# Another order of the seven products of a tile pair, with all of their sums taken out of PSUM by VectorE, in a one-layer hybrid decoder step

## The chip, the cores and the metric

The kernel runs on one core of a Trainium2 chip. The metric is the device time of one execution in microseconds, as the median of several runs. Times of single instructions and waits come from one profiled execution.

## What is computed

One inference step of one decoder layer for a prompt of 2048 tokens with 16 meta tokens, and for 8 sample sequences of 8 tokens. All is fp32, with a model width of 1024.

```python
def _in_proj(x, g_pre, w_in, b_in):
    h = _rmsnorm(x, g_pre)
    p = jnp.einsum('btd,dc->btc', h, w_in) + b_in
    return jnp.split(p, np.cumsum(IN_WIDTHS)[:-1].tolist(), axis=-1)
...
def _mlstm_chunk(carry, inp):
...
    Wqk = W * jnp.einsum('blhd,bshd->bhls', q, k)
    num = a[..., None] * jnp.einsum('blhd,bhde->bhle', q, C0) + jnp.einsum('bhls,bshe->bhle', Wqk, v)
...
def _merge(x, att, hm, za, om, zm, ga, gb, w_pa, w_pb, w_out, g_post):
    y_a = att * jax.nn.silu(za)
    y_m = jax.nn.sigmoid(om) * hm * jax.nn.silu(zm)
    merged = jax.nn.sigmoid(ga) * jnp.einsum('btc,cd->btd', y_a, w_pa) + jax.nn.sigmoid(gb) * jnp.einsum('btc,cd->btd', y_m, w_pb)
    out = jnp.einsum('btd,de->bte', merged, w_out)
    return x + _rmsnorm(out, g_post)
```

Branch A is sliding-window attention with sinks (16 query heads, 4 key heads), branch B an mLSTM with 4 heads of width 256, in chunks of 128 tokens.

## The kernel before

**Split numbers.** Every projection is computed from numbers in two parts: an fp32r upper part and the rest, the lower part. A product of two such numbers is three matmuls: upper by upper, upper by lower, lower by upper. ScalarE writes the upper part (a copy), VectorE or GpSimd subtracts it from the number to give the lower part.

**First stage** (`attention`). The tokens lie in 17 tiles (tile 0: meta and sample rows). Four passes over them, one for each key head, make 68 slots m = 0 to 67, each with the projection of the next tile, the scores, softmax and values of this one. In pass 0 h is made, split and stored in DRAM as `hh_t`. From slot 17 on the split h of tile m+2 is loaded in SP's slot m (`load_split`, L283, two DMAs of 512 KB) into one of two buffers, behind what SP did in the slot before. GpSimd makes beside that the sums of operands for the later pairs (`operand_sums`, stored at L603 as `sh_t`), sixteen sets of weight differences (stored at L590) and the lower parts of the first weight units (`early_units`). In its last slots TensorE makes the first four products of the stream (`first_products`, L1552 to L1554). A barrier of all engines closes the stage.

**Stream** (`stream`). Ten passes ZM, H0 to H3, GA, PA, GB, PB, OUT, each with a weight of 1024 x 1024. An item is tile 0 alone (4 products) or a pair of tiles (7 products), so a pass has 4 + 8 x 7 = 60 products, and the stream 600, numbered q. A product is an operand of 128 x 512 by a weight block of 512 x 512, 12 matmuls of 512 columns (L2790, L2792, L2793). The two tiles of a pair times the four blocks of the weight would be 8 products. A scheme of the Strassen and Winograd kind makes 7 of them out of sums of operands and differences of weight blocks (T1 to T4), and sums the results. P1 and P2 give c11, the left half of row 0; c12 is its right half, c21 and c22 are row 1. Before, the order is P1, P5, P6, P2, P7, P3, P4. bank_first takes P1 and P2, bank_third P5 and then P3, bank_second P6, then P7 afresh, then P4 on top.

Who takes what out before: VectorE takes t1 (after P1), u2 (P6), c11 (P2), c12 (P3) and c21 (P4); ScalarE copies p5 (L2464) and p7 (L2469); GpSimd adds in `second_sums` (L2264, L2267) and `last_sum` (L2275, c22). `c` has three lines: line 2 for tile 0, lines 0 and 1 for the rows of a pair. Before a line is written, `wait_line` waits until its former contents are stored (ZM, GA, PA, GB), used by the mixer (head passes), transposed (PB) or added by GpSimd (OUT).

**Operands.** The passes called STREAMED (ZM, the head passes, GA, GB) load split operands from DRAM, three products ahead. PA, PB and OUT (SUMMED) load raw tiles. There ScalarE makes the upper parts (L2329), VectorE the lower ones (L2507), GpSimd the operand sums (`make_sums`, L2209 to L2221).

**Weights.** A pass needs 28 units of 128 x 512, split at 2 for each product from 6 products before the pass to 8 products into it (`SPLITS_AT`): ScalarE the upper part (L2336), VectorE (L2512) or GpSimd (L2179) the lower one. Units of T1 to T4 are read from `difs_t`. For passes 2 to 9 GpSimd makes the differences in the stream (`differences`, L2186 to L2192), in 64 steps spread by `DIF_AT` over products 1 to 331. SP loads (L1991) and stores them (L1995).

**Mixer.** In a head pass each tile is turned (`TURN`: transposes of q and k), scored one product later (`SCORE`) and mixed two products later (`MIX`). All engines walk the same list of products in order. The order within one engine at one product is that of the code.

## Time and profile before

| | us |
|---|---|
| median of 3 runs | 2965.0 (2960.8 to 2971.6) |
| the profiled execution | 2957.5 |
| its span, first to last instruction | 2955.7 |
| TensorE busy | 2758.2 (93%) |
| VectorE busy | 1551.9 (53%) |
| ScalarE busy | 1014.8 (34%) |
| GpSimd busy | 1232.4 (42%) |
| mean granted TensorE clock | 0.976 |

PE is TensorE, PEld its weight loads, DVE VectorE, ACT ScalarE, POOL GpSimd, and SPq the queue of SyncE, which issues DMAs. The first stage lasts to about 941 us. The passes of the stream begin at 924 (ZM), 1124, 1362, 1596, 1829 (H0 to H3), 2062 (GA), 2234 (PA), 2403 (GB), 2572 (PB) and 2758 us (OUT). L12 is line 12 of the kernel before.

### The profile page before, as it was taken

Reading aid. Unit: us, or ns where it says so; the run is one execution under the profiler, and the core shown is the slowest. Engines: PE = TensorE matmul, PEld = TensorE weight load, DVE = VectorE, ACT = ScalarE, POOL = GpSimd, SP = SyncE. Lnnn points to the kernel's source line nnn. Section 1 sums busy time; section 2 is a strip of 40 time slices with the busy share of each in tenths; the row PEclk is TensorE's granted clock in tenths of the full one; section 3 lists DMA queues with packets and bytes.
Section 4 is the critical chain, followed back from the end, with each engine's and each line's share of the span. In section 5 each row is a group of like instructions: output and inputs, shape, how many; then the busy total and the mean of one; then the engine's idle time right before and its main releaser. Section 6 shows DMA issues by size and latency. Waiting matters only on the chain. (4 is left out here: it accounts for less than half of the span.)

```text
span 2955.7 us, 46918 instructions
## 1 busy us (share of the span) xinstructions
PE 2758.2 (93%) x15620; PEld 2306.7 (78%) x15620; DVE 1551.9 (53%) x3788; ACT 1014.8 (34%) x2451; POOL 1232.4 (42%) x1386
## 2 busy tenths in 40 slices
PE   6999898899886998999999999999999999999798
PEld 5888787788775875887788788788887878778686
DVE  5775555455443114446446446545317551487887
ACT  5774333333333002224124123223214341343443
POOL 3343433433444333234234224324425452377777
PEclk9999999999898999999999999999999999999999
DMA  8664555454456998888888788778987577966643
GB/s 305 236 205 144 166 187 184 154 181 158 160 173 209 306 332 291 272 281 278 252 278 300 242 268 290 251 232 276 335 302 260 186 256 249 307 213 221 200 154 145
DMA packets 410017, 697.49 MB, mean 236 GB/s; under 512 B 31778, under 2 KB 176551, under 8 KB 409748
## 3 DMA queue, kind: packets, MB, share of 16 engines
q1 hardware_dynamic: 394628, 649.42, 66.4%
q10 hardware_dynamic: 12432, 35.76, 3.4%
q0 software_dynamic: 2720, 9.32, 1.0%
q8 instruction: 128, 2.10, 0.3%
q14 instruction: 109, 0.89, 0.1%
HBM read 526.87 MB, written 169.48 MB: 236 GB/s over the span
## 5 line engine op out<-in xcount | busy, mean ns | idle before, releaser
L2790 PE MATMUL bank_second<-w_all,a_all 128*128 128x512 f32 x704 | 287.3, 408 | 17.8 <-POOL w_all L2179 10.2
L2793 PE MATMUL bank_second<-w_all,a_all 128*128 128x512 f32 x704 | 276.0, 392 | 0.0
L2792 PE MATMUL bank_second<-w_all,a_all 128*128 128x512 f32 x704 | 275.1, 391 | 0.0
L2275 POOL TENSOR_TENSOR st_c<-st_p 128x512 f32<-128x512 f32 x80 | 107.7, 1347 | 331.1 <-PE st_bank_u L2842 257.8
L2790 PE MATMUL bank_first<-w_all,a_all 128*128 128x512 f32 x560 | 226.0, 404 | 19.3 <-DVE st_c L2531 16.3
L2264 POOL TENSOR_TENSOR st_t<-st_u,st_db 128x512 f32<-128x512 f32 x56 | 73.6, 1314 | 394.1 <-DVE st_u L2558 394.0
L2793 PE MATMUL bank_first<-w_all,a_all 128*128 128x512 f32 x560 | 219.2, 391 | 0.0
L2792 PE MATMUL bank_first<-w_all,a_all 128*128 128x512 f32 x560 | 218.9, 391 | 0.0
L316 PE MATMUL bank_third<-w_all,a_all 128*128 128x256 f32 (+1 forms) x480 | 158.3, 330 | 59.2 <-DMA a_all<-hh_t 58.9
L2405 ACT ACTIVATE mx_qkt<-st_bank_t 128x512 f32<-128x512 f32 x68 | 40.7, 599 | 445.5 <-PE st_bank_t L2813 445.5
L307 PE MATMUL bank_first<-w_all,a_all 128*128 128x384 f32 x544 | 189.3, 348 | 0.0
L2790 PE MATMUL bank_third<-w_all,a_all 128*128 128x512 f32 x440 | 178.8, 406 | 7.8 <-issue 3.5
L309 PE MATMUL bank_first<-w_all,a_all 128*128 128x384 f32 x544 | 182.0, 335 | 0.0
L308 PE MATMUL bank_first<-w_all,a_all 128*128 128x384 f32 x544 | 182.0, 335 | 0.0
L923 ACT ACTIVATE at_sm<-at_sm,at_nmx 128x208 f32<-128x208 f32 x272 | 124.5, 460 | 166.4 <-DVE at_nmx L1131 166.3
L769 POOL TENSOR_TENSOR at_vbc<-at_qkv,at_ones 64x64 f32<-64x64 f32 x68 | 23.8, 349 | 370.3 <-PE at_bank_po L1475 370.3
L2507 DVE TENSOR_TENSOR a_all<-h_raw,a_all 128x512 fp32r<-128x512 f32 x99 | 134.6, 1359 | 76.5 <-ACT a_all L2329 75.9
L2790 PEld LDWEIGHTS bank_second<-w_all,a_all 128*128 128x128 f32 x704 | 132.9, 189 | 52.6 <-POOL w_all L2179 9.2
L2793 PE MATMUL bank_third<-w_all,a_all 128*128 128x512 f32 x440 | 172.2, 391 | 0.0
L2792 PE MATMUL bank_third<-w_all,a_all 128*128 128x512 f32 x440 | 171.5, 390 | 0.0
L2512 DVE TENSOR_TENSOR w_all<-st_waiting,w_all 128x512 fp32r<-128x512 f32 x129 | 122.8, 970 | 76.7 <-ACT w_all L2336 76.3
L2336 ACT ACTIVATE w_all<-st_waiting 128x512 fp32r<-128x512 f32 x188 | 114.1, 628 | 128.8 <-DMA st_waiting<-difs_t 59.5
(383 smaller groups left out, 7760.5 us busy)
## 6 DMA issues: line engine op xcount, KB each, us to landing
a_all<-hh_t SPq DMA_DIRECT2D x284, 512.0 KB, 5.6
a_all<-sh_t SPq DMA_DIRECT2D x224, 512.0 KB, 5.2
st_waiting<-difs_t SPq DMA_DIRECT2D x152, 256.0 KB, 6.9
h_raw<-l_blocks_in SPq DMA_DIRECT2D x64, 512.0 KB, 7.0
difs_t<-h_raw SPq DMA_DIRECT2D x64, 512.0 KB, 6.9
st_waiting<-l_blocks_in SPq DMA_DIRECT2D x108, 256.0 KB, 6.7
hh_t<-a_all SPq DMA_DIRECT2D x34, 512.0 KB, 6.1
st_raw<-y_t ACTq DMA_DIRECT2D x16, 1024.0 KB, 6.4
```

Of the source, the lines that this page charges most:

```text
L307: nc.tensor.matmul(out, hi[:, j], k.w_hi[:, j, col:col + n], start=(j == 0), stop=False)
L308: nc.tensor.matmul(out, hi[:, j], k.w_lo[:, j, col:col + n], start=False, stop=False)
L309: last = nc.tensor.matmul(out, lo[:, j], k.w_hi[:, j, col:col + n], start=False, stop=(j == KT - 1))
L316: nc.tensor.matmul(out, hi[:, j], k.w_hi[:, j, col:col + n], start=(j == 0), stop=False)
L923: nc.scalar.activation(sm[:, g, :], sm[:, g, :], ACT.Exp, bias=nmx[:, g:g + 1], scale=HD ** -0.5, accum_out=rs[:, g:g + 1]).then_inc(exp_r ...
L2275: G.tensor_tensor(c[:, 1, LW:D], p5[:, :], p7[:, :], ALU.add).then_inc(c22_ready, 1)
L2336: A.activation(unit_half(v, 0), unit_view(v), ACT.Copy).then_inc(k.upper_done, 1)
L2507: V.tensor_tensor(k.a_all[:, 1, q % NA], operand(q), hi, ALU.subtract).then_inc(a_lo, 1)
L2512: V.tensor_tensor(unit_half(v, 1), unit_view(v), unit_half(v, 0).bitcast(F32), ALU.subtract).then_inc(lower_done_dve, 1)
L2790: T.matmul(bank_view(bank, at), hi, weight_row(k, at, 0, t), start=fresh and t == 0, stop=False, skip_group_check=True)
L2792: T.matmul(bank_view(bank, at), hi, weight_row(k, at, 1, t), start=False, stop=False, skip_group_check=True)
L2793: last = T.matmul(bank_view(bank, at), lo, weight_row(k, at, 0, t), start=False, stop=t == KH - 1, skip_group_check=True)
```

## The change

- The pair's order is P1, P6, P5, P7, P2, P3, P4, with the weight order to match. P7 is accumulated in bank_second on top of P6.
- VectorE takes out all: t2 and t1 from P1 (t1 by ScalarE in PA, PB and OUT), u2 from P6, u3 and c22 after P7, c11, c12, c21. P3 waits for c22. The two ScalarE copies and GpSimd's `second_sums`, `last_sum` and `make_db` are gone.
- `make_sums` is moved from GpSimd to VectorE as it stands.
- In the first stage ScalarE loads the split h, of tile m+3 in slot m, behind the four at_pt copies, and the first four operands of the stream as well.
- The early weight units come one slot earlier. The last four no longer wait for the lower parts of the others.
- The bias of ZM is loaded before the barrier into the first half of h_raw, and VectorE takes the right half of tile 0 out there into the second half.
- The 64 difference steps are moved to products 64 to 299 and their DMAs to ScalarE's queue. A load waits for the landing of the store two steps before, a store for GpSimd's step.
- The tiles of a head pass are turned earlier: a pair's at its P3 and at the next P1 (before: at the next P1 and the next P2).
- The units of the ZM pass are split 5 products later, and the first six units of a next pass are loaded 6 products later.
- On VectorE the outputs of the mixer now stand before its next weights, queries and gates.

```diff
-NEEDED = (T3, B22, B11, B21, T1, T2, T4)
-RELEASED = (B11, T1, T2, B21, T3, B22, T4)
+NEEDED = (T3, B22, B11, B21, T2, T1, T4)
+RELEASED = (B11, T2, T1, T3, B21, B22, T4)
...
-            if m < KVH * NT - NT + 2:
+            if m < KVH * NT - NT + 1:
...
             def slot(a, t, m, u, half):
-                if m + 2 == NT:
-                    sp.wait_ge(hh_out[0], 32 * (NT // 2 + 1))
-                    sp.wait_ge(hh_out[1], 32 * (NT // 2))
-                if NT <= m + 2 < KVH * NT:
-                    load_split(sp, k, m + 2, u, (m + 2) % NT)
-                elif m + 2 == KVH * NT:
+                if m == KVH * NT - 3:
+                    sp.wait_ge(pair_out[1], 32 * (NPT // 2 + 1))
+                    sp.dma_start(k.h_raw[:, 0].rearrange("p j n -> p (j n)"), k.l_bias[0:1].to_broadcast([P, D])).then_inc(k.first_bias_in, 16)
+                if m == KVH * NT - 1:
                     sp.wait_ge(proj_a, m + 1)
-                    sp.wait_ge(pair_out[1], 32 * (NPT // 2 + 1))
-                    for q in range(2):
-                        load_operand(sp, k, q)
-                elif m + 2 > KVH * NT:
-                    sp.wait_ge(proj_a, m + 1)
-                    sp.wait_ge(k.lower_done, EARLY - KH)
                     for e in range(EARLY - KH, EARLY):
                         load_early(e)
-                    for q in range(2, 4):
-                        load_operand(sp, k, q)
...
                     nc.scalar.activation(pt[:, g, :], pbank(g)[:, 0:2 * P], ACT.Copy).then_inc(pt_ready, 1)
+                n = m + 3
+                if n == NT:
+                    act.wait_ge(hh_out[0], 32)
+                    act.wait_ge(hh_out[1], 32 * (NT // 2))
+                elif n == NT + 1:
+                    act.wait_ge(hh_out[0], 32 * (NT // 2 + 1))
+                if NT <= n < KVH * NT:
+                    load_split(act, k, n, n % 2, n % NT)
+                elif KVH * NT <= n < KVH * NT + 2:
+                    act.wait_ge(proj_a, n - 1)
+                    act.wait_ge(pair_out[1], 32 * (NPT // 2 + 1))
+                    for q in (0, 1) if n == KVH * NT else (2, 3):
+                        load_operand(act, k, q)
...
             all_steps(KVH, slot)
+            dve.wait_ge(k.prod, 2)
+            dve.wait_ge(k.first_bias_in, 16)
+            dve.wait_ge(pair_out[1], 32 * (NPT // 2 + 1))
+            V.tensor_tensor(k.h_raw[:, 1, KH:KT].rearrange("p j n -> p (j n)"), k.bank_first[:, :],
+                            k.h_raw[:, 0, KH:KT].rearrange("p j n -> p (j n)"), ALU.add).then_inc(k.first_ready, 1)
...
-P1, P5, P6, P2, P7, P3, P4 = range(7)
-PAIR_BLOCK = (B11, T1, T2, B21, T3, B22, T4)
+P1, P6, P5, P7, P2, P3, P4 = range(7)
+PAIR_BLOCK = (B11, T2, T1, T3, B21, B22, T4)
...
-DIF_AT = {c: 1 + (c - DIF_FIRST) * 21 // 4 for c in range(DIF_FIRST, N_DIF)}
+DIF_AT = {c: N_PROD * H0 + 4 + ((c - DIF_FIRST) * 9 // 2 if c < DIF_FIRST + 8 else 37 + (c - DIF_FIRST - 8) * 18 // 5) for c in range(DIF_FIRST, N_DIF)}
...
     if t < 3:
-        return b + (6, 13, 16)[t]
-    return b + N_SINGLE + N_PAIR * ((t + 1) // 2) + (0 if t % 2 else 3)
+        return b + (4, 11, 12)[t]
+    return b + N_SINGLE + N_PAIR * (t // 2) + (5 if t % 2 else 0)
...
+            def load_dif(c):
+                if c - DIF_FIRST >= 2:
+                    act.wait_ge(dif_out[c % 2], 16 * ((c - DIF_FIRST) // 2))
...
+            def store_dif(c):
+                act.wait_ge(dif_step, 4 * (c - DIF_FIRST + 1))
...
+                if q + 3 in DIF_NOW:
+                    load_dif(DIF_NOW[q + 3])
+                if q - 3 in DIF_NOW:
+                    store_dif(DIF_NOW[q - 3])
                 mixer_first(q)
...
                 if j == P1 and s in STREAMED:
...
+                    V.tensor_tensor(t2[:, :], bank_x[:, :], bias_of(s)[:, LW:D], ALU.add).then_inc(t2_ready, 1)
+                    V.tensor_tensor(t1[:, :], bank_x[:, :], bias_of(s)[:, 0:LW], ALU.add).then_inc(t1_ready, 1)
...
+                elif j == P7:
+                    dve.wait_ge(c22_ready, m)
+                    V.tensor_tensor(u3[:, :], bank_y[:, :], t2[:, :] if s in STREAMED else t1[:, :], ALU.add).then_inc(u3_ready, 1)
+                    wait_line(dve, g, 1, 1)
+                    dve.wait_ge(u3_ready, m + 1)
+                    V.tensor_tensor(c[:, 1, LW:D], bank_z[:, :], u3[:, :], ALU.add).then_inc(c22_ready, 1)
...
-                    fresh = j in (P1, P5, P6, P7)
+                    fresh = j in (P1, P5, P6)
...
                     elif j == P3:
-                        pe.wait_ge(p5_ready, m + 1)
+                        pe.wait_ge(c22_ready, m + 1)
                     elif j == P4:
-                        pe.wait_ge(p7_ready, m + 1)
+                        pe.wait_ge(u3_ready, m + 1)
```

## Rows read from the trace of the kernel before

**Rows 1.** Busy time by stretch: length; PE, PEld, DVE, ACT, POOL; clock; DMA share, GB/s.
```profile
234.00:924.00 690.00, 611.68 (x5009) 545.46 (x5007) 357.05 (x1482) 262.98 (x902) 264.29 (x498) 0.94 0.52 167
...
1596.00:1829.00 233.00, 231.65 (x1124) 187.42 (x1123) 120.83 (x270) 63.64 (x151) 80.28 (x82) 1.00 0.83 270
...
2572.00:2758.00 186.00, 178.03 (x842) 147.12 (x841) 154.80 (x126) 81.04 (x145) 134.55 (x91) 1.00 0.67 229
2758.00:2956.00 198.00, 169.99 (x737) 139.38 (x735) 153.26 (x141) 83.70 (x155) 146.47 (x76) 0.94 0.44 157
```
**Rows 2.** Timeline of TensorE, first matmuls of two products in ZM: start, duration.
```profile
1033.22 0.39 PE L2790 MATMUL bank_second<-w_all,a_all 128*128 128x512 f32 x1
...
1035.94 0.39 PE L2790 MATMUL bank_first<-w_all,a_all 128*128 128x512 f32 x1
```
**Rows 3.** Waits of TensorE, whole run: us in total, times, longest.
```profile
PE bank_third L316 <- DMA a_all<-hh_t: 58.9, 25, 5.9
PE bank_first L2790 <- DVE st_c L2531: 16.3, 1, 16.3
...
PE bank_second L2790 <- POOL w_all L2179: 10.2, 3, 7.7
...
PE st_bank_t L2740 <- POOL st_c L2241: 7.6, 2, 6.1
...
PE bank_third L2790 <- DMA a_all<-sh_t: 6.6, 2, 4.2
...
PE bank_first L1552 <- issue: 4.4, 1, 4.4
```
**Rows 4.** Line L898, once a slot: from 234 to 924 us, then 472 to 493.
```profile
L898 ACT ACTIVATE at_qt<-at_bank_pt x52: 384/385/387, 234.2 to 917.8; 128x256 f32<-128x256 f32 x52
...
L898 ACT ACTIVATE at_qt<-at_bank_pt x2: 385/386/386, 472.8 to 492.6; 128x256 f32<-128x256 f32 x2
```
**Rows 5.** Timeline of ScalarE, two slots; in brackets idle time before, and its releaser.
```profile
602.03 0.39 ACT L898 ACTIVATE at_qt<-at_bank_pt 128x256 f32<-128x256 f32 x1 [2.41 <-PE at_bank_pt L1414]
...
613.06 0.39 ACT L898 ACTIVATE at_qt<-at_bank_pt 128x256 f32<-128x256 f32 x1 [1.93 <-PE at_bank_pt L1414]
```
**Rows 6.** Waits of SP's queue from 234 to 924 us.
```profile
SPq L603 <- POOL h_raw L835: 194.0, 17, 20.5
```
**Rows 7.** Line L283, the loads of split h, from 234 to 924 us.
```profile
DMA to landing us min/median/max: 3.3/6.0/9.1
```
**Rows 8.** Timelines of TensorE and of SP from 940 to 963 us.
```profile
957.77 0.77 PE L2790 MATMUL bank_first<-w_all,a_all 128*128 128x512 f32 x1 [16.31 <-DVE st_c L2531]
...
943.15 2.97 SPq L2001 DMA_DIRECT2D st_waiting<-difs_t  x6
```
**Rows 9.** DMA issues of the page: count, KB, median us from issue to landing.
```profile
st_waiting<-difs_t SPq DMA_DIRECT2D x152, 256.0 KB, 6.9
...
difs_t<-h_raw SPq DMA_DIRECT2D x64, 512.0 KB, 6.9
...
zm_t<-st_c SPq DMA_DIRECT2D x17, 512.0 KB, 7.7
...
gb_t<-st_c SPq DMA_DIRECT2D x17, 512.0 KB, 6.4
```
**Rows 10.** Eviction of P1 (busy, mean ns); timelines of VectorE and GpSimd in PB.
```profile
L2551 DVE TENSOR_TENSOR st_t<-bank_first,st_bias 128x512 f32<-128x512 f32 x56 | 38.7, 691 | 96.9 <-PE bank_first L2793 96.9
...
2653.04 2.30 DVE L2507 TENSOR_TENSOR a_all<-st_raw,a_all 128x512 fp32r<-128x512 f32 x1
...
2659.93 0.68 DVE L2507 TENSOR_TENSOR a_all<-h_raw,a_all 128x512 fp32r<-128x512 f32 x1
...
2652.00 2.79 POOL L2241 TENSOR_TENSOR st_c<-st_c,st_e 128x1024 f32<-128x1024 f32 x1 [2.01 <-DVE st_c L2518]
```
**Rows 11.** Transposes in PB (timeline); GpSimd's add in OUT (busy, mean ns).
```profile
2657.35 0.60 PE L2740 MATMUL st_bank_t<-ident,st_c 128*128 128x128 f32 x4
...
L2247 POOL TENSOR_TENSOR st_e<-st_c,st_e 128x1024 f32<-128x1024 f32 x17 | 43.3, 2547 | 37.1 <-DVE st_c L2592 34.0 <-ACT st_p L2464 3.0
```

More of the change, by code:

```diff
@@ L605, in load_early @@
             def load_early(e):
+                if e == 2 * KH:
+                    for out in dif_out:
+                        sp.wait_ge(out, 16 * KH)
                 sp.dma_start(early_place(e), unit_source(k, EARLY_ORDER[e]).rearrange("p (t n) -> p t n", n=P)).then_inc(early_in[e % 4], 16)
@@ L1763, in stream @@
         sums = k.h_raw[:, :, :, :].rearrange("p u (s j) n -> p (u s) j n", j=KH)
-        t1, u2, p5, p7 = (sb(name, [P, LW]) for name in ("t1", "u2", "p5", "p7"))
-        bias, db = sb("bias", [P, D]), sb("db", [P, LW])
+        t1, t2, u2, u3 = (sb(name, [P, LW]) for name in ("t1", "t2", "u2", "u3"))
+        bias = sb("bias", [P, D])
+        first = k.h_raw[:, 1].rearrange("p j n -> p (j n)")
         c = sb("c", [P, 3, D + 1])
@@ L2530, in evict_single @@
                     wait_bias(s)
-                    V.tensor_tensor(c[:, 2, cols], bank[:, :], bias[:, cols], ALU.add).then_inc(ready, 1)
+                    V.tensor_tensor(c[:, 2, cols] if g else first[:, cols], bank[:, :], bias_of(s)[:, cols], ALU.add).then_inc(ready, 1)
                 elif s == OUT:
@@ L2580, in evict_pair, with make_sums @@
                     wait_line(dve, g, 1, 0)
-                    V.tensor_tensor(c[:, 1, 0:LW], bank_y[:, :], u2[:, :], ALU.add).then_inc(c21_ready, 1)
+                    dve.wait_ge(t1_ready, m + 1)
+                    V.tensor_tensor(c[:, 1, 0:LW], bank_y[:, :], t1[:, :], ALU.add).then_inc(c21_ready, 1)
+            def make_sums(g, which):
+                n = sums_before(g)
+                if g == N_ITEM * PA and which == 0:
+                    for out in dif_out:
+                        dve.wait_ge(out, 16 * ((N_DIF - DIF_FIRST) // 2))
+                if which == 0 or is_single(g):
+                    wait_raw(dve, g)
+                if is_single(g):
+                    if which == 0:
+                        dve.wait_ge(a_lo, sums_taken(g, 0))
+                        V.tensor_tensor(sums[:, 0], raw_block(g, 0, 0), raw_block(g, 0, 1), ALU.add).then_inc(sums_ready, 1)
+                elif which == 0:
+                    dve.wait_ge(a_lo, sums_taken(g, 0))
+                    V.tensor_tensor(sums[:, 0], raw_block(g, 1, 0), raw_block(g, 1, 1), ALU.add).then_inc(sums_ready, 1)
+                    dve.wait_ge(sums_ready, n + 1)
+                    dve.wait_ge(a_lo, sums_taken(g, 1))
+                    V.tensor_tensor(sums[:, 1], sums[:, 0], raw_block(g, 0, 0), ALU.subtract).then_inc(sums_ready, 1)
+                else:
+                    dve.wait_ge(a_lo, sums_taken(g, 2))
+                    V.tensor_tensor(sums[:, 2], raw_block(g, 0, 0), raw_block(g, 1, 0), ALU.subtract).then_inc(sums_ready, 1)
+                    dve.wait_ge(sums_ready, n + 2)
+                    dve.wait_ge(a_lo, sums_taken(g, 3))
+                    V.tensor_tensor(sums[:, 3], raw_block(g, 0, 1), sums[:, 1], ALU.subtract).then_inc(sums_ready, 1)
             def norm_row(g, row):
@@ L2695, in _ @@
                             evict_single(g, j)
+                h = META.get(q - 1)
+                if h is not None:
+                    meta(h)
+                n = MIX.get(q - 1)
+                if n is not None:
+                    outputs(n)
                 n = SCORE.get(q - 1)
@@ L2700, in _ @@
                     split_operand(q + 3)
+                if 0 <= q < Q_ALL:
+                    s, i, j = place(q)
+                    g = N_ITEM * s + i + 1
+                    if g < G_ALL and g // N_ITEM in SUMMED:
+                        if j == (1 if i else 0):
+                            make_sums(g, 0)
+                        if j == (4 if i else 2):
+                            make_sums(g, 1)
                 n = TURN.get(q - 1)
```

187 lines of the change are left out of this document (48 added, 139 removed).

## The prediction

> **What bounds the kernel now.** Three views in this order. The busy table by stretch [rows 1] says where TensorE is the limit: in the middle of the run it is busy 231.65 of 233 us (a head pass) at full clock, but only 612 of 690 us in the first stage, at 0.94 of the clock, 178 of 186 us in the PB pass and 170 of 198 us in the OUT pass with its tail. So a product pass has nothing to give in its steady part: two products of one pair start at 1033.22 and 1035.94, 2.72 us apart, matmul behind matmul [rows 2], and a change can only harm there. What there is to gain is idle time, and the list of TensorE's waits [rows 3] says whose it is: 58.9 us in 25 waits for the split h (hh_t) in the attention stage, 16.3 us once at the start of the stream, 10.2 and 7.6 us for GpSimd at pass starts, 6.6 us for operand loads, 4.4 us once before the first products.
>
> The 58.9 us cost more than themselves. The ScalarE copy L898 runs once a slot: 52 times from 234.2 to 917.8 [rows 4], 51 slots in 683.6 us. A slot without a wait takes 613.06 - 602.03 = 11.03 us [rows 5]; a first-tile slot without one 492.6 - 472.8 = 19.8 us [rows 4], and there are 3. 48 x 11.03 + 3 x 19.8 = 588.8, so 94.8 us are lost: the waits and the half clock (1.2 GHz) behind them. Why are the loads late? SP's own waits [rows 6]: it stands 194 us in 17 waits before the pair stores at L603, for GpSimd, and the hh_t load is queued behind them. The landing itself takes 3.3 to 9.1 us, median 6.0 [rows 7].
>
> **Split h from ScalarE's queue.** The load of tile m+3 is now issued in ScalarE's slot m behind the four at_pt copies; its TensorE wait (projection of m+2) precedes the transposes those copies read, so ScalarE does not stop for it. That is before the end of slot m; the tile is first needed at the start of slot m+2, so a whole clean slot (11.03 us) lies between. Two issues, estimated at 0.5 us each from SP's six in 2.97 us [rows 8], then at most 9.1: 10.1 us, so it arrives. The issues stand before the at_gt copy; ScalarE then sits idle for 1.93 us before the next L898 copy [rows 5], so 1 us fits. What is next late is nothing I can see: a slot without the wait is all TensorE. I take -90 of the -94.8 us, bounds -60 and -95. At one end DMA traffic pressed into shorter slots makes some loads late, at the other none.
>
> In front of this stands a rule. The Trainium skill, "DMA: Bandwidth & Descriptors", section "Issuing engines are not separate DMA queues", says that DMAs of all issuing engines share the same 16 DMA engines and that spreading them saves only the time of initiating. By that rule alone the 90 us would be near zero; it hangs on whether landing or issue is late, and rows 6 and 7 show the issue.
>
> **The early units one slot earlier** remove the 4.4 us before the first products [rows 3], which are w_early lowered by GpSimd behind a difference set: -4 (0 to -8).
>
> **Start of the stream.** TensorE ends at 957.77 - 16.31 = 941.46 and begins again at 957.77 [rows 8], when VectorE has read both banks of the single tile, which waits for the bias behind four lowerings. Now one half of that tile is taken out before the barrier, the bias is already there, and P1 and P6 have weights and operands. The third product needs T1, loaded after the barrier: six issues from 943.15 [rows 8], then the median of 6.9 us of the loads of difference units [rows 9] and a split and lowering of some 2 us: about 951 to 952. By then two products (5.4 us) are done, where before none was: it corresponds to a start at about 946. -11 (-7 to -14).
>
> **Weight differences out of the ZM pass, onto ScalarE's queue.** Relief for the operand loads, which wait 6.6 us on one row [rows 3] and a few more on others, around the burst of state and unit loads: -6 (0 to -12). The 64 differences now fall on products 64 to 299. For most, the load of c+2 stands one product behind the store of c on the same engine and waits for its landing, 6.9 us too [rows 9]; a head-pass product averages 233/60 = 3.9 us, so ScalarE is held some 3 us. Queued behind are the copies and exponentials of the mixer. I price it at 0: ScalarE is busy 64 of 233 us [rows 1], and it runs ahead of TensorE in the products between two tiles. Upper bound in the rivals.
>
> **VectorE takes all sums from PSUM.** Per streamed pair three evictions more (t2, u3, c22), else two, at 691 ns each [rows 10] (PSUM operand, so the same beside GpSimd); gone are ScalarE's two copies and GpSimd's sums. 56 x 3 + 24 x 2 = 216 x 0.69 = 149 us on an engine that is 52% busy; hidden, if they come in time. Each is waited for with one product between, 2.72 us, and the worst slot has two, 1.4 us: on time. In PA, PB and OUT 4 operand sums a pair come too, 33 x 0.69 = 23 us a pass. VectorE is busy 155 of 186 us in PB [rows 1], which looks full. But an a_all lowering there takes 2.30 us beside GpSimd's L2241 and 0.68 with GpSimd idle [rows 10]: GpSimd loses six pieces of 512 a pair, at half of L2247's 2547 ns for 1024 [rows 11] some 61 of its 135 us in PB, and with them about half of what lengthens VectorE. I work with 155 + 23 + 11 - 35 = 154 us: no new bound.
>
> What is new is **what c22 waits for.** It must find its line free, VectorE waits in order, and P3 waits for it. (a) PB: the line is freed by the transposes of the former pair, which TensorE makes after P2, the product just before P3. They start at 2657.35, the first four take 0.60 us [rows 11]; only behind them can VectorE write c22 (0.69 + about 0.1 us), with TensorE idle: 0.8 x 7 pairs = +5.6 us, sure. u3, P2's eviction and the lowerings queued behind c22 have some 7 us of room. (b) OUT: the line is freed by GpSimd's add (2547 ns) [rows 11] behind the norm of the row (1.3 to 2.1 us) behind one lowering: 0.69 + 0.16 + 1.3 + 2.55 = 4.7 us of the 4.75 that are there, up to 1.6 us too late: +4 (0 to 11). (c) ZM, GA, GB: by the store of the line, issued behind an operand load, some 0.5 us into the third product; it may take 3 x 2.72 - 0.5 - 0.69 = 7.0 us, and takes 7.7 in ZM and 6.4 in GB [rows 9]; without differences ZM should be like GB: +2 (0 to 8).
>
> **Order in the head passes.** A pair's tiles are turned at P3 and at the next P1, mixed two products later; tile 2 one product behind tile 1. VectorE's slot after P1 then holds two evictions, the outputs and the queries, near 4.5 us, in a slot of 2.72 us plus a mix and a turn: fits. T1's lowering meets the queries of tile 0. +3 (0 to 12).
>
> **Pass starts PB and OUT.** GpSimd loses the sums before its lowerings: 10.2 + 7.6 = 17.8 us of waits [rows 3], and the OUT stretch stands at 0.94 of the clock [rows 1]. VectorE still has lowerings, sums and evictions there at once. -12 (+4 to -22).
>
> **The sum.** -90 - 4 - 11 - 6 - 12 + 5.6 + 4 + 2 + 3 = -108. The profiled execution took 2957.5 us (span 2955.7 and 1.8 around it), so 2849. It lies 7.5 us under the median of the runs, 2965.0; the same 108 off that is **2857 us**.
>
> **Rivals.**
> 1. The hh_t loads stay late on the other queue, because the landing grows. Against: 6.0 us median against more than 11 us of room. For: traffic of 690 us falls into some 600. Half of the gain gone: 2857 + 45 = 2902; all of it, as by the rule of the skill's page: 2947. Chance 0.14, nearly all on the half.
> 2. VectorE becomes the bound in PA, PB and OUT: the lengthening stays (155 + 34 = 189 us in PB against 186) and c22's wait of some 3.5 us a pair adds to it. That is 189 + 8 x 3.5 = 217 against 186 in PB and OUT, and nothing gained at their starts: +31 x 2 + 12 = 74, so 2931. Chance 0.06.
> 3. Slower than before: ScalarE's hold at the difference loads. 56 of them, 3 us each, is 168 us; if all reach TensorE, 2857 + 168 = 3025. It decides at the point where ScalarE comes to a load less than 3 us before the copy of the turned tile is due. The profile speaks against it, as two or three products of each pair ask nothing of ScalarE. A third of it would still be faster. Chance 0.04.
> 4. The change does not do what it says (a wait I read wrongly puts the load back behind GpSimd, gains and losses cancel): 2957 to 2974. Chance 0.02.
>
> My forecast keeps 0.74, its own range 2828 to 2888. For 8 in 10 I take in half of rival 1: **2822 to 2905**. Within 0.3% (9 us) a measurement of this kernel can't tell a change from none. Faster 0.94, same 0.02, slower 0.04.
>
> **What the profile after would show.** The wait for hh_t gone, L898 at 11.0 us a slot, the first stage done near 825; the idle time at the stream's start 2 to 3 us, then some 2 to 3 more before the third product; in PB idle pieces of 0.8 us before P3 released by VectorE; lowerings of a_all mostly at 0.69 us; PA, PB and OUT no longer than 170, 190 and 190 us. It is wrong if hh_t waits remain at a third of the tiles, if head passes last over 240 us, or if TensorE waits for VectorE in most pairs of ZM, GA and GB.

## The result and the profile after

The changed kernel takes 2919.9 us (median of 4 runs, 2916.6 to 2923.5), the kernel before beside it 2968.3. The ratio is 0.984 with a 95% interval of 0.9815 to 0.9865. So it is 48 us faster, where I had forecast 108, and 2919.9 lies above my range of 2822 to 2905. Direction right, size wrong.

The head of the page after:

```profile
span 2914.8 us, 46458 instructions
...
PE 2763.5 (95%) x15620; PEld 2298.4 (79%) x15620; DVE 1636.7 (56%) x4103; ACT 936.0 (32%) x2291; POOL 762.2 (26%) x1064
```

TensorE's waits over the whole run (us in total, times, longest; from here on line numbers are those of the kernel named):

```profile
PE bank_third L2760 <- DVE st_c L2497: 27.4, 21, 3.4
PE st_bank_s L2772 <- ACT mx_yt L2379: 12.5, 4, 3.1
...
PE st_bank_n L2839 <- DVE mx_wqk L2564: 10.0, 4, 4.9
PE bank_third L2760 <- POOL w_all L2177: 9.2, 2, 4.9
```

The 58.9 us for split h [rows 3] are gone, and so are the 16.3 us at the start of the stream. In their place stand waits of the new order: L2497 writes c22, L2379 takes out the transposed y of a tile, L2564 makes a tile's weights. The ScalarE copy once a slot (L898 before, L892 now) for the first stage:

```profile
L892 ACT ACTIVATE at_qt<-at_bank_pt x52: 373/384/384, 233.8 to 841.7; 128x256 f32<-128x256 f32 x52
```

That is 607.9 us for the 51 slots that took 683.6 [rows 4]; 588.8 would be clean. The table sets lengths side by side, each from the first matmul of a pass to that of the next, as span of the rows by stretch. The last two columns are kernels of the experiments.

| us | before | after | first half alone | after, repaired |
|---|---|---|---|---|
| 51 slots | 683.6 | 607.9 | 608.2 | 607.1 |
| last slot copy to the stream's product 4 | 40.0 | 17.7 | 18.8 | 19.4 |
| rest of ZM | 166.5 | 164.7 | 162.7 | 165.7 |
| four head passes | 937.3 | 969.2 | 935.4 | 935.3 |
| GA, PA, GB | 510.2 | 516.1 | 513.5 | 523.4 |
| PB | 186.0 | 193.1 | 189.0 | 184.2 |
| OUT | 186.7 | 201.2 | 186.7 | 184.6 |
| span | 2955.7 | 2914.8 | 2858.3 | 2864.5 |

Items 0 and 1 below are the first eleven products of a head pass, items 2 and 3 the next fourteen, each sum over the four passes, read from the first matmuls of their products in TensorE's timeline.

So 98 us were gained by product 4 of the stream (75.7 in the slots, 22.3 behind them), and some 57 of them were given back from there to the end: 31.9 in the head passes, 14.5 in OUT, 7.1 in PB and 5.9 in GA, PA and GB are 59.4, less the 1.8 that the rest of ZM is shorter. The second head pass and OUT by stretch, after (columns as in [rows 1]):

```profile
1264.99:1508.41 243.42, 234.15 (x1124) 188.62 (x1122) 130.33 (x294) 54.94 (x134) 61.36 (x75) 0.99 0.85 279
...
2702.45:2903.67 201.22, 178.35 (x737) 141.24 (x735) 140.49 (x180) 73.82 (x136) 55.65 (x26) 0.94 0.43 147
```

TensorE sits idle for 9 us in the head pass, where before a head pass had 1.35 [rows 1], and the clock is under 1.00. VectorE is busy 130 of 243 us, so it is not the bound. Where in these passes does the time go?

**Tiles 1 and 2 of a head pass.** Rows of TensorE, VectorE and ScalarE from 1084 us, product 13 of H0; the same idle time of 3.1 us stands there in all four head passes.

```profile
1088.61 1.03 PE L2808 MATMUL st_bank_n<-mx_cn,mx_qat 128*128 128x257 f32 x4
...
1094.05 0.41 PE L2772 MATMUL st_bank_s<-ident,mx_y 128*128 128x128 f32 x2 [3.12 <-ACT mx_yt L2379]
...
1096.25 0.63 PE L2762 MATMUL bank_second<-w_all,a_all 128*128 128x512 f32 x1
```
```profile
1090.27 0.42 DVE L2577 TENSOR_TENSOR mx_qat<-mx_qkt,mx_rows 128x256 f32<-128x256 f32 x1 [3.92 <-PE st_bank_n L2809]
...
1092.32 0.48 DVE L2622 SCALAR_TENSOR_TENSOR mx_y<-st_bank_n,mx_den,mx_tz 128x256 f32<-128x256 f32 x1
```
```profile
1090.97 0.51 ACT L2349 ACTIVATE mx_kw<-st_c,spare 128x256 f32<-128x256 f32 x1 [4.27 <-PE st_bank_u L2812]
1092.92 0.42 ACT L2366 ACTIVATE mx_to<-st_c 128x256 f32<-128x256 f32 x1 [1.43 <-DVE mx_y L2622]
1093.24 0.40 ACT L2367 ACTIVATE mx_tz<-mx_z 128x256 f32<-128x256 f32 x1
1093.55 0.36 ACT L2379 ACTIVATE mx_yt<-st_bank_s 128x256 f32<-128x256 f32 x1
```

Nobody is busy here; it is a chain. Tile 2 is turned one product behind tile 1. VectorE's queries of tile 2 (L2577) wait for the mix of tile 1, ScalarE's k (L2349) for its state update, its tanh (L2366) for VectorE's y, and its copy of the y of the tile before (L2379) stands behind all of that, with TensorE waiting for it. Behind the idle time the matmuls of 512 columns take 0.63 us instead of 0.39: the granted clock is 0.61 in the mean from 1094.0 to 1098.4 us and 1.00 again from 1098.6 on. That is the half clock, 1.2 GHz, for some 3 us.

**ScalarE held by a difference load.** ScalarE's rows around the start of H2, then TensorE's:

```profile
1504.74 0.40 ACTq L2266 DMA_DIRECT2D difs_t<-h_raw  x1
...
1514.14 0.38 ACTq L2262 DMA_DIRECT2D h_raw<-l_blocks_in  x1
1514.56 0.31 ACT L2333 ACTIVATE mx_wexp<-mx_wexp 128x128 f32<-128x128 f32 x1 [3.33 <-DMA difs_t<-h_raw]
```
```profile
1515.31 1.22 PE L2808 MATMUL st_bank_n<-mx_cn,mx_qat 128*128 128x257 f32 x2 [3.91 <-DVE mx_wqk L2564]
```

The store is issued at 1504.74 and the load that waits for its landing at 1514.14; the exponential queued behind the load starts after 3.33 us of idle time, then come VectorE's weights, then TensorE. The stores (L2266) in the whole run:

```profile
DMA to landing us min/median/max: 2.9/7.3/15.5
```

In the head passes ScalarE stands idle for 39.4 us in 11 such waits, the longest 6.3 us. That is less than the 56 waits of 3 us of my bound, but not nothing.

**c22 in PB and OUT.** One pair of each, VectorE (in OUT with GpSimd) and TensorE:

```profile
2584.49 0.60 PE L2711 MATMUL st_bank_s<-ident,st_c 128*128 128x128 f32 x4
2585.96 0.47 PE L2760 MATMUL bank_third<-w_all,a_all 128*128 128x512 f32 x1 [0.88 <-DVE st_c L2497]
```
```profile
2585.12 0.69 DVE L2497 TENSOR_TENSOR st_c<-bank_third,st_u 128x512 f32<-128x512 f32 x1 [2.91 <-PE st_bank_s L2711]
```
```profile
2757.93 2.50 DVE L2432 TENSOR_TENSOR a_all<-h_raw,a_all 128x512 fp32r<-128x512 f32 x1
...
2761.14 1.29 DVE L2555 SCALAR_TENSOR_TENSOR st_c<-st_c,st_small,st_e 128x1024 f32<-128x1024 f32 x1
...
2764.90 0.69 DVE L2497 TENSOR_TENSOR st_c<-bank_third,st_u 128x512 f32<-128x512 f32 x1 [1.87 <-POOL st_e L2215]
```
```profile
2762.51 2.36 POOL L2215 TENSOR_TENSOR st_e<-st_c,st_e 128x1024 f32<-128x1024 f32 x1 [2.63 <-DVE st_c L2555]
```
```profile
2765.74 0.47 PE L2760 MATMUL bank_third<-w_early,a_all 128*128 128x512 f32 x1 [1.86 <-DVE st_c L2497]
```

In PB c22 starts when the transposes have ended, 0.88 us too late, in all seven pairs from the second on. In OUT it starts when GpSimd's add has ended, and TensorE waits 1.9 us in six pairs and 0.8 in the last.

### The profile page after: what moved, and what is told of

Its sections match the earlier page's. It is cut to its first block and busy times, and to the rows that moved or that the text cites. A ratio compares the mean times of both kernels' runs of the same rounds, so it can differ in the third digit from the quotient of the medians.

```text
span 2914.8 us, 46458 instructions
## 1 busy us (share of the span) xinstructions
PE 2763.5 (95%) x15620; PEld 2298.4 (79%) x15620; DVE 1636.7 (56%) x4103; ACT 936.0 (32%) x2291; POOL 762.2 (26%) x1064
## 5 line engine op out<-in xcount | busy, mean ns | idle before, releaser
L2760 PE MATMUL bank_second<-w_all,a_all 128*128 128x512 f32 x736 | 298.9, 406 | 2.0 <-DVE st_u L2491 0.9
L2763 PE MATMUL bank_second<-w_all,a_all 128*128 128x512 f32 x736 | 288.6, 392 | 0.0
L2762 PE MATMUL bank_second<-w_all,a_all 128*128 128x512 f32 x736 | 288.3, 392 | 0.0
L2177 POOL TENSOR_TENSOR w_all<-st_waiting,w_all 128x512 fp32r<-128x512 f32 x59 | 80.1, 1359 | 626.4 <-ACT w_all L2274 626.4
L2760 PE MATMUL bank_third<-w_all,a_all 128*128 128x512 f32 x464 | 190.3, 410 | 29.9 <-DVE st_c L2497 12.9
L2760 PE MATMUL bank_first<-w_all,a_all 128*128 128x512 f32 x496 | 197.5, 398 | 4.1 <-DMA a_all<-first_t 2.0
L2763 PE MATMUL bank_first<-w_all,a_all 128*128 128x512 f32 x496 | 194.6, 392 | 0.0
L2762 PE MATMUL bank_first<-w_all,a_all 128*128 128x512 f32 x496 | 194.6, 392 | 0.0
L2184 POOL TENSOR_TENSOR h_raw<-h_raw 128x256 f32<-128x256 f32 x64 | 48.5, 757 | 538.4 <-DMA h_raw<-l_blocks_in 538.2
L2763 PE MATMUL bank_third<-w_all,a_all 128*128 128x512 f32 x464 | 184.6, 398 | 0.0
L2762 PE MATMUL bank_third<-w_all,a_all 128*128 128x512 f32 x464 | 184.4, 397 | 0.0
L2760 PEld LDWEIGHTS bank_second<-w_all,a_all 128*128 128x128 f32 x736 | 139.6, 190 | 34.5 <-issue 6.8
L2763 PEld LDWEIGHTS bank_second<-w_all,a_all 128*128 128x128 f32 x736 | 139.1, 189 | 30.1
L2762 PEld LDWEIGHTS bank_second<-w_all,a_all 128*128 128x128 f32 x736 | 139.5, 190 | 26.8
L316 PE MATMUL bank_third<-w_all,a_all 128*128 128x256 f32 (+1 forms) x480 | 147.3, 307 | 0.2 <-POOL a_all L297 0.2
L2494 DVE TENSOR_TENSOR st_u<-bank_second,st_t 128x512 f32<-128x512 f32 x80 | 55.2, 690 | 157.3 <-PE bank_second L2763 157.3
```

The costliest lines, as they stand in the source:

```text
L316: nc.tensor.matmul(out, hi[:, j], k.w_hi[:, j, col:col + n], start=(j == 0), stop=False)
L2177: G.tensor_tensor(unit_half(v, 1), unit_view(v), unit_half(v, 0).bitcast(F32), ALU.subtract).then_inc(k.lower_done, 1)
L2184: G.tensor_tensor(d[:, R11], d[:, R12], d[:, R11], ALU.subtract).then_inc(dif_step, 1)
L2494: V.tensor_tensor(u3[:, :], bank_y[:, :], t2[:, :] if s in STREAMED else t1[:, :], ALU.add).then_inc(u3_ready, 1)
L2760: T.matmul(bank_view(bank, at), hi, weight_row(k, at, 0, t), start=fresh and t == 0, stop=False, skip_group_check=True)
L2762: T.matmul(bank_view(bank, at), hi, weight_row(k, at, 1, t), start=False, stop=False, skip_group_check=True)
```

## The experiments

Theory: the first half of the change (queue of split h, early units, bias ahead of the barrier) gives what I forecast, and the second half gives 57 us back in the places above. Rival: VectorE, with three more evictions a pair, is simply late. Ratios are against the kernel before, times are medians of 4 runs, and what is said of single passes comes from the profiled one of them.

**1. The load of split h alone.** In the kernel before:

```diff
-                if m + 2 == NT:
...
-                    load_split(sp, k, m + 2, u, (m + 2) % NT)
...
+                n = m + 3
...
+                if NT <= n < KVH * NT:
+                    load_split(act, k, n, n % 2, n % NT)
                 act.wait_ge(gate_tr, m + 1)
```

> The kernel before, with one edit of the change: ScalarE loads the split h of tile m+3 in slot m, behind the four at_pt copies; all else stays, SP's loads of the first operands too. My theory: this edit alone carries the gain of the first stage. L898 comes 17 to 67 in about 600 us instead of 672.6, TensorE's waits for hh_t there go from 58.9 us to under 5, nothing is given back in the stream, so the kernel is 75 us faster: 2890 (2880 to 2900). That would make it faster than the whole change. Rival A (the gain needs the other edits of the stage as well): 2905 to 2935. Rival B (the landing is what is late, so another queue saves only the issuing time): 2955 to 2965.

Measured: 2880.4 us, ratio 0.971 (0.969 to 0.974). That is 10 us better than I expected, and this one edit is faster than the whole change by 40 us. Its slots, and its loads from 234 to 850 us:

```profile
L893 ACT ACTIVATE at_qt<-at_bank_pt x52: 375/384/385, 233.5 to 839.1; 128x256 f32<-128x256 f32 x52
```
```profile
L283 ACTq DMA_DIRECT2D a_all<-hh_t x98: 366/465/1630, 242.3 to 815.5; - x98
...
DMA to landing us min/median/max: 3.2/5.0/10.2
```

605.6 us for 51 slots, 78.0 less, and no wait for hh_t in them. A landing takes 5.0 us in the median against 6.0 [rows 7], with a longest of 10.2: hardly faster, but no longer issued late. The Trainium skill ("DMA: Bandwidth & Descriptors", section "Issuing engines are not separate DMA queues") says that another issuing engine saves only the initiating. The landings here agree. But what "initiating" was worth is 78 us. By the rows it was late because it stood behind another wait, 194 us in 17 times [rows 6]; the loads left on SP's queue but ahead of those waits, which would show this without another queue, were not run.

**2. The differences back on SP's queue**, in the kernel after (SP's side is shown; the same lines are taken out of ScalarE's loop):

```diff
                     next_operand(q + LOADED_AHEAD)
+                if q + 3 in DIF_NOW:
+                    load_dif(DIF_NOW[q + 3])
+                if q - 3 in DIF_NOW:
+                    store_dif(DIF_NOW[q - 3])
```

> The kernel after, with the loads and stores of the weight differences in the stream issued by SP, behind the operand load, instead of ScalarE. My theory: ScalarE's hold at a difference load, which waits for the landing of a store, is what makes TensorE wait 3.9 us at product 180, 3.6 us at product 245 and 2.7 us of the 4.9 us at product 126. These go, with the half clock behind them: head passes 0 to 8 us shorter, 2905 (2900 to 2912). Rival A (VectorE with its three more evictions is late in the head passes, whatever ScalarE does): the same waits stay, 2920. Rival B (SP, held at the same waits, now brings the operands late): slower than 2920, with waits for hh_t and sh_t in the head passes.

Measured: 2917.2 us, ratio 0.983 (0.981 to 0.986): too high for my theory, and level with the change. The waits at products 180 and 245 are gone (3.9 to 1.0 us, and 3.6 to none), and the head passes take 963.0 us instead of 969.2. But at product 126 TensorE still waits 3.7 us. SP's queue says why:

```profile
1280.39 0.69 SPq L1636 DMA_DIRECT2D a_all<-sh_t  x1
1287.69 0.38 SPq L2007 DMA_DIRECT2D h_raw<-l_blocks_in  x1
```

For 7 us SP issues nothing, standing at the same wait, and behind it the weight units of H1 come late. In the head passes SP stands 124.6 us in 42 of these waits. So the hold comes from the short distance between the two commands, and moving them from ScalarE's queue to SP's only changed what stood behind it.

**3. Tile 1 turned one product earlier**, in the kernel after:

```diff
-        return b + (4, 11, 12)[t]
+        return b + (4, 10, 12)[t]
```

> The kernel after, with tile 1 of each head pass turned one product earlier (10 instead of 11 products into the pass), so that tiles 1 and 2 are two products apart instead of one. My theory: turned one product apart, tile 2's queries wait for tile 1's mix and then everything behind them runs in series; that is the idle time of 3.1 us at product 13 of each of the four head passes, and the half clock behind it. Both go: item 2 of a head pass falls from 31.7 to about 27 us, 2900 (2896 to 2906). Rival A (the time is bound to the 16 matmuls of the mixer in that product, or moves into the sample updates at products 7 to 10): 2918 to 2922. Rival B (VectorE is overloaded there): the wait stays with VectorE as its releaser, 2915 to 2920.

Measured: 2905.1 us, ratio 0.979 (0.976 to 0.981). The waits for L2379 are gone altogether, item 2 takes 26.5 us instead of 31.5 to 31.7 in all four passes, and the head passes 952.2 us instead of 969.2: 17.0 (the medians are 14.9 apart). VectorE's work is the same in both, so the chain was the cause.

**4. PB's row 1 transposed behind P7**, in the kernel after:

```diff
-                    g = ended(q - 1 - 3 * row, row)
+                    g = ended(q - 1 - 2 * row, row)
                     if g is not None and g // N_ITEM == PB:
                         transposes(g, row)
```

> The kernel after, with the transposes of row 1 in PB made one product earlier, behind P7 instead of behind P2. My theory: c22 then finds its line free before TensorE is through with P2, so the 0.88 us ahead of P3 go in all seven pairs, and with them the rest of what the pair takes over 20.85 us: 7 x 1.1 = 8 us, 2912. PB falls from 193 to about 185 us. Rival A (GpSimd's add for row 1 ends later than P7, and TensorE waits for it instead): PB unchanged or longer, 2920 or more. Rival B (the 0.88 us are VectorE's own length for u3 and c22 behind P2's lowerings, not the line): the wait stays, 2918 to 2920.

Measured: 2910.1 us, ratio 0.981 (0.979 to 0.983). PB by stretch (length; PE, PEld, DVE, ACT, POOL; clock, DMA share, GB/s), after and then here:

```profile
2509.38:2702.45 193.07, 182.06 (x841) 149.12 (x840) 141.93 (x178) 73.57 (x129) 63.48 (x42) 0.98 0.67 222
```
```profile
2509.12:2694.72 185.60, 179.75 (x842) 148.26 (x840) 141.95 (x178) 73.34 (x129) 63.24 (x42) 0.99 0.69 229
```

7.5 us, and pairs of 20.9 us as in the kernel before.

**5. OUT's row 1 normed into the bias buffer**, in the kernel after:

```diff
-                V.scalar_tensor_tensor(out=c[:, at, 0:D], in0=c[:, at, 0:D], ...
+                V.scalar_tensor_tensor(out=bias[:, :] if row else c[:, at, 0:D], in0=c[:, at, 0:D], ...
...
-                    G.tensor_tensor(e[:, row], c[:, at, 0:D], e[:, row], ALU.add)
+                    G.tensor_tensor(e[:, row], bias[:, :] if row else c[:, at, 0:D], e[:, row], ALU.add)
```

> The kernel after, where in OUT the norm of row 1 writes its result into the bias buffer, free in that pass, and GpSimd adds from there. Line 1 is free when VectorE's norm is through (before c22 in its own order), not when GpSimd's add of 2.4 to 2.5 us behind it is. My theory: that add is what c22 waits for in OUT. The 1.9 us ahead of P3 in six pairs, and the half clock that follows, go: six pairs of 21.4 to 23.1 us become 19.0 to 19.3, the last one 19.3: 20 us, 2900 (2896 to 2906). Rival A (VectorE itself is late there, with norm, two lowerings and two evictions): pairs of 20 to 21 us, 2908 to 2914. Rival B (the wait is for ScalarE's mean square): unchanged.

Measured: 2905.2 us, ratio 0.980 (0.979 to 0.982). OUT takes 184.4 us instead of 201.2, its pairs 19.7 us instead of 21.4 to 23.1 (19.0 in the kernel before). 16.8 us of the 20: the wait ahead of P3 is 0.1 us. Why 0.7 us a pair remain is open.

**6. Operand sums back on GpSimd**, in the kernel after: `make_sums` with `G` for `V`, at its old place in GpSimd's loop.

> The kernel after, with the operand sums of PA, PB and OUT made by GpSimd again, at the places they had in the kernel before. My theory: moving them to VectorE paid, because GpSimd's work beside VectorE lengthens VectorE's lowerings. Back on GpSimd the a_all lowerings go from 0.7 back to about 2 us, VectorE comes later to c22, and P3 waits longer: PB and OUT together 5 to 20 us longer, 2925 to 2940. Rival (the lengthening costs nothing, VectorE has room): 2917 to 2923, PB and OUT within 2 us.

Measured: 2926.1 us, ratio 0.988 (0.985 to 0.991), 6 us more than the kernel after, with runs from 2922.8 to 2937.7 us beside 2916.6 to 2923.5. The profiled run is the slowest of these, at 2937.7, so the lengths of its passes say too much: PA, PB and OUT are 2.8, 2.0 and 9.8 us longer in it. In PB and OUT the lowerings of a_all from raw tiles (busy, mean ns), after and then here:

```profile
L2432 DVE TENSOR_TENSOR a_all<-st_raw,a_all 128x512 fp32r<-128x512 f32 x52 | 37.7, 725 | 33.6 <-ACT a_all L2252 33.6
```
```profile
L2465 DVE TENSOR_TENSOR a_all<-st_raw,a_all 128x512 fp32r<-128x512 f32 x52 | 71.6, 1376 | 37.7 <-ACT a_all L2285 37.6
```

The lowerings of sums (h_raw) in the same passes hardly differ, 1221 ns against 1293. In PB VectorE is busy 141.9 us with the sums and 154.6 without them: with more to do it is through sooner. Moving the sums to VectorE seems to have paid, by some 6 us, but the two kernels' intervals (0.9815 to 0.9865, and 0.985 to 0.991) overlap. The Trainium skill ("SBUF — State Buffer", section "SBUF: two separate sides") says that VectorE reading two SBUF inputs and GpSimd lock each other out for a whole instruction; 1376 against 725 ns agrees in direction.

**7. Difference loads later, steps 4.5 products apart**, in the kernel after:

```diff
-DIF_AT = {c: N_PROD * H0 + 4 + ((c - DIF_FIRST) * 9 // 2 if c < DIF_FIRST + 8 else 37 + (c - DIF_FIRST - 8) * 18 // 5) ...
+DIF_AT = {c: N_PROD * H0 + 4 + (c - DIF_FIRST) * 9 // 2 ...
...
-                if q + 3 in DIF_NOW:
-                    load_dif(DIF_NOW[q + 3])
+                if q + 1 in DIF_NOW:
+                    load_dif(DIF_NOW[q + 1])
```

> The kernel after, differences still on ScalarE's queue, but each difference load is issued 1 product ahead of its step instead of 3, and the steps stand 4.5 products apart all along (now 3.6 for most). From a store to the load of the same buffer it is then 5 products instead of 1.2 to 3, more than a landing of 7 to 10 us, so that nobody is held. My theory: ScalarE's holds are gone, and SP isn't held instead as in the run with the loads on SP. Items 0 and 1 of the four head passes, 224.7 us together (216.5 with the loads on SP), fall to about 210, the kernel to 2906 (2900 to 2912). Rival A (what is late there is the traffic itself, 345 GB/s at a DMA share of 0.95 in 1265 to 1305): 216 to 225, 2915 to 2920. Rival B (GpSimd is now the one that waits for the landing, and its unit lowerings come late at pass starts): waits for GpSimd's w_all, 2915 to 2930.

Measured: 2917.2 us, ratio 0.984 (0.982 to 0.986). Half right. Items 0 and 1 of the head passes fall to 209.0 us and the head passes to 953.2, 16.0 less, and ScalarE waits for no landing of a difference store there any more. Two things were changed at once, the distance and the spacing of the steps; run 9 parts them. But GA takes 185.7 us instead of 176.3, since the last steps now fall there. VectorE in a pair of GA, and TensorE behind it:

```profile
2031.55 0.69 DVE L2497 TENSOR_TENSOR st_c<-bank_third,st_u 128x512 f32<-128x512 f32 x1 [3.66 <-DMA ga_t<-st_c]
```
```profile
2032.39 0.56 PE L2760 MATMUL bank_third<-w_all,a_all 128*128 128x512 f32 x1 [2.57 <-DVE st_c L2497]
```

c22 waits for the store of its line, in seven pairs of GA, 10.8 us in all. That is a weak spot of the new order: it needs each store landed within a pair, and difference traffic beside it (329 GB/s here, 286 after) breaks that.

**8. The first half of the change alone**: edit 1, and to it the early units, the first operands from ScalarE's queue, bias and right half of tile 0 ahead of the barrier, the units of ZM 5 products later, and the differences out of ZM (on SP's queue, 4.5 products apart; in the change they are on ScalarE's and mostly 3.6 apart). The pair's order and all behind it as before.

> The kernel before with the first half of the change: split h and the first four operands from ScalarE's queue, early units one slot earlier, bias of ZM and right half of tile 0 before the barrier, units of ZM 5 products later, and the differences out of ZM, but on SP's queue, one every 4.5 products from product 64. The order of the pair's products, who takes the sums out, the tiles' turns, the operand sums and all of PB and OUT stay as before. My theory: all of the gain is in this half, and all that is given back is in the other: 2880 of the run with the load alone, less 16 at the start of the stream and 2 to 6 in ZM: 2860 (2852 to 2868), the head passes 233 to 237 us as before. Rival A (differences pressed into fewer products hold SP and make operands and units late, in this order of products too): head passes 236 to 242, 2870 to 2885. Rival B (the start of the stream gains only with the new order, since here P5 needs T1 second): 2870 to 2880.

Measured: 2862.5 us, ratio 0.966 (0.964 to 0.968). Faster than both kernels, by 101 us than the one before. The head passes take 935.4 us, OUT 186.7, as before. My terms for this half were -90, -4, -11 and -6, which is 111 us; 101 came. So 2857, forecast for the whole, nearly fits this half alone, but only because my terms for the other half were to cancel (+2.6).

**9. The kernel after with all repairs**: edits 3, 4 and 5, and the load one product ahead of its step as in 7, the steps where the change has them.

> The kernel after with all four repairs: tile 1 turned 10 products into a head pass, row 1 of PB transposed behind P7, row 1 of OUT normed into the bias buffer, and each difference load 1 product ahead of its step instead of 3 (the steps themselves stay at products 64 to 299, none in GA's later pairs). My theory: these four places are all that the second half of the change gives back, so their sizes add: 20 + 7.5 + 17 (from the pass lengths of the single runs) and 15 for the holds in the head passes = 60 off 2920: 2861 (2853 to 2870), level with the kernel with the first half alone, 2862. Rival A (the losses have one common cause, traffic, and taking one away brings up another): 2875 to 2890. Rival B (the new order has a gain of its own under its losses, in PB's and OUT's starts): 2845 to 2853.

Measured: 2867.1 us, ratio 0.967 (0.965 to 0.968). 53 of the 57 us come back, so the four places nearly add up (17.0, 7.5, 16.8 and 16.0 are 57.3), and neither rival holds. Against the first half alone (2862.5 us, 0.964 to 0.968) no difference is shown. With the steps where the change has them and only the loads later, items 0 and 1 of the head passes fall from 224.7 to 211.4 us; the turn of tile 1 alone had not shortened them (228.4 in run 3), so some 13 us there were the holds. GB takes 175.9 us here and 170.3 in the kernel after, with the same code in it; in the kernels with the new order GB lies anywhere from 170.3 to 175.9 us, with the waits for its stores, so 3 us in a pass are no effect of an edit. Items 0 and 1 of the head passes are slower in the new order (211.4 us against 198.9), items 2 and 3 faster (208.9 against 219.3).

**10. The same with half of the unit lowerings on GpSimd:**

```diff
-    return kt != 3 if s - 1 in STREAMED else kt % 2 == 1
+    return kt % 2 == 1
```

> The same, and besides that half of the weight units' lower parts in the passes behind a streamed one made by GpSimd, where it was one of four (VectorE makes the other half). My theory: what is left in items 0 and 1 of a head pass is VectorE late for tile 0, which the new order turns two products earlier while VectorE makes three of four lower parts; with a lighter VectorE the wait at the sample rows falls by 1 us a pass, in all 3 to 8 us off the run before. Rival (GpSimd is the late one, behind its difference steps, at 1.4 us a piece against 0.7): 2 to 15 us more, with waits for GpSimd's w_all.

Measured: 2880.0 us, ratio 0.972 (0.970 to 0.973): 13 us slower, where I expected 3 to 8 faster. The time is in the rival's range, but its sign is missing: the waits for GpSimd's w_all are 10.0 us here and 9.7 in the repaired kernel. TensorE's wait at the sample rows, repaired kernel and then this one:

```profile
PE st_bank_n L2844 <- DVE mx_wqk L2569: 9.3, 4, 2.9
```
```profile
PE st_bank_n L2844 <- DVE mx_wqk L2569: 13.6, 4, 4.4
```

It grows. VectorE is busy 129.9 us of H1 instead of 132.2, for seven pieces fewer, so seven lowerings on GpSimd free it for 2.3 us where they take some 4.8 at 0.69 each. What the rest of the 13 us is stays open.

**11. Kernel 8 with the differences at the change's products**, loads one product ahead.

> The kernel with the first half of the change, differences at the products of the change (64 to 299, none in GA's later pairs), each load 1 product ahead of its step, on SP's queue. My theory: GA was 5.5 us longer there than in the run with the load alone because its last difference steps met the stores of ga_t and the raw loads of PA; with none there, GA is at 172 us: 2857 (2852 to 2862). Rival (3.6 products apart, SP waits for the landing of a store ahead of the operand loads): head passes 236 us and more, 2865 to 2880.

Measured: 2871.0 us (2861.9 to 2876.4), ratio 0.968 (0.965 to 0.970). GA falls from 177.4 to 174.1 us, over half of the way to the 172 that I expected, but the head passes rise from 935.4 to 944.4: the rival. The steps at the change's products cost the head passes more than they save in GA. Whether it is their spacing or the later load is not shown, since both differ from run 8.

**12. The repaired kernel with tile 0 turned at product 5, tile 1 at 11:**

```diff
-        return b + (4, 10, 12)[t]
+        return b + (5, 11, 12)[t]
```

> The repaired kernel with one thing other: in each head pass tile 0 is turned 5 products into the pass instead of 4, and so tile 1 at 11 again (the sample updates now lie in products 8 to 11) with tile 2 at 12. The tiles 1 and 2 are one product apart as in the kernel after, which by the run on them costs 5 us a pass in item 2; that is known and isn't the question. The question is items 0 and 1 of the four head passes: 211.4 us together in the repaired kernel, 198.9 in the kernel with the first half alone (tile 0 turned at 6). My theory: what is left there is the turn of tile 0, which now meets VectorE's lowerings of the weight units; a product later it is 203 to 208. Rival (VectorE's three more evictions a pair are late there whatever the turn): 210 to 213. Total: 2867 + 20 - 5 = 2882 by mine, 2887 by the rival.

Measured: 2880.3 us, ratio 0.972 (0.970 to 0.975). Items 0 and 1 take 206.8 us instead of 211.4. Some 1.4 of the 4.6 are the transposes of tile 1 (0.36 us a pass), which moved out of item 1, so the later turn is worth about 3 us. With passes varying by 3 us it points my way and no more, and does not reach the 198.9 of the old order; what the remaining 8 us are stays open. Item 2 goes back to 31.1 to 33.1 us, which shows once more what one product between two tiles costs.

## Why the prediction was wrong, point by point

- **Split h, -90 (-60 to -95).** Right in kind, within its bounds: -75.7, and -78.0 with that edit alone. 19 us above clean slots stay: 4.7 in the three first-tile slots (64.1 us against 59.4), 5.5 in one slot with a wait of 2.0 us for ScalarE at a clock of 0.79, the rest in smaller pieces, none of them a wait for hh_t. Rival 1, and with it the rule of the Trainium skill ("DMA: Bandwidth & Descriptors", section "Issuing engines are not separate DMA queues") taken alone, does not come about.
- **Early units and start of the stream, -4 and -11.** Together -22.3, more than the sum of 15. TensorE waits 2.0 us at the start and 3.6 us ahead of the third product, which I had at 2 to 3 each; but the latter is a wait for an operand (`sh_t`), not for the T1 units that I had in mind.
- **Differences onto ScalarE's queue, hold priced at 0.** This step failed. It was my rival 3, with the right place and a chance of 0.04, but I ruled it out on an average: a landing of 6.9 us and a product of 3.9. The landings went up to 15.5 us, with a median of 7.3, and the two or three free products of a pair did not cover them at the starts of passes. Measured: 39.4 us of idle time on ScalarE, and some 13 to 16 us of the kernel's time by runs 9 and 7, against 168 in the bound.
- **Order in the head passes, +3 (0 to 12).** This step failed too. I counted the work in VectorE's slot and found room; what ended last was no engine's work but the chain from tile 1 to tile 2. Measured by the run on it: 17.0 us, 3.1 us of idle time and some 2 of half clock a pass. In part it replaced losses of the old order in items 2 and 3 (219.6 us for both in four passes; 229.6 in the kernel after; 208.9 with the repair). The head passes last 240.9 to 243.4 us; over 240 was one of my signs of being wrong, and it came.
- **c22 in PB, +5.6.** Right: 0.88 us a pair, and 7.5 us with all that goes with it.
- **c22 in OUT, +4 (0 to 11).** The mechanism was right and the term mis-sized: 16.8 by run 5. I had the add as up to 1.6 us too late in some pairs. It is 1.9 us late in six, since, by the rows, a lowering ahead of the norm takes 2.50 us beside GpSimd's add for row 0 instead of 0.68, and in three pairs of 23.0 to 23.1 us the half clock comes on top (mean clock 0.93, and 1.00 in the pairs of 21.4 to 21.5).
- **c22 in ZM, GA and GB, +2 (0 to 8).** In these the waits ahead of P3 for L2497 sum to 27.4 - 18.3 = 9.1 us (18.3 of them lie in PB and OUT), in 7 of 24 pairs, and GA, PA and GB together are 5.9 us longer. A little above.
- **Pass starts PB and OUT, -12 (+4 to -22).** Items 0 and 1 of PB: 38.4 to 38.2 us, of OUT: 53.2 to 47.4. About -6, half of it.
- **VectorE no new bound.** Right: 141.9 of 193.1 us in PB, where I had 154; rival 2 fell.

From -108, with the -12 for pass starts halved between PB and OUT: +14 (slots), -7 (start), +3 (ZM), +29 (head passes), +5 (GA to GB), +7 (PB), +16 (OUT) gives -41, the difference of the spans. Two thirds of the error are the head passes and OUT. The range was too narrow for the same reason: the hold stood at 0 with its bound only among the rivals, and in bounding the waits one by one I left out the half clock that follows some of them.

## What to carry to other kernels

When an instruction with a wait is moved to another queue, ask how far it stands behind the thing it waits for, at the place where that distance is shortest, not on average; the hold goes with it to any queue. When steps of neighbouring tiles are brought closer, follow one tile's chain to the next through all engines, since room on every engine says nothing about it. And time a change of several parts part by part: here one half, with the differences 4.5 products apart on SP's queue, was worth 101 us, and the other half took 57 of them back.

## What the runs showed of the hardware

- A short idle time costs more than itself. Behind 3.1 us at product 13 matmuls took 0.63 instead of 0.39 us for some 3 us. In OUT the same wait of 1.9 us stands in three pairs of 21.4 to 21.5 us, at a clock of 1.00, and in three of 23.0 to 23.1 us, at 0.93.
- A store of 512 KB landed in 7.3 us in the median and in 15.5 at most. One issued at 1504.74 let its successor go only at 1514.14, 9.4 us later; in that stretch the DMA engines moved 366 GB/s at a share of 0.99.
- Less work on GpSimd is worth time to VectorE: 725 ns for a lowering from raw tiles against 1376 with the sums on GpSimd, in PB and OUT.
